# Feed-forward with 512-column moving operands and the down projection one output block at a time

## The reference

```python
def swiglu(x, w_gate, w_up, w_down):
    return (jax.nn.silu(x @ w_gate) * (x @ w_up)) @ w_down

x = x + 0.5 * swiglu(rms_norm(x, ffn1_norm[l]), ffn1_w_gate[l], ffn1_w_up[l], ffn1_w_down[l])
...
x = x + 0.5 * swiglu(rms_norm(x, ffn2_norm[l]), ffn2_w_gate[l], ffn2_w_up[l], ffn2_w_down[l])
```

## Time and profile before

| what | value |
|---|---|
| time, median of 3 runs | 1132.12 us (1131.58 to 1132.88) |
| span of the profiled execution | 1131.7 us, 22927 instructions |
| what lies around that span | the execution's own time is not given apart; the median of the runs is 0.4 us above the span |
| PE busy | 1110.8 us, 98% |
| DVE busy | 756.4 us, 67% |
| ACT busy | 572.3 us, 51% |
| POOL busy | 81.4 us, 7% |
| mean granted TensorE clock | 0.995 of full speed (2.4 GHz) |
| weight stream | 369 blocks of 512 KB, median 3.5 us from issue to landing |

### The profile page before, as it was taken

One profiled execution on the slowest core, in us unless ns is written; L12 is line 12 of the kernel. 1 busy time (PEld: TensorE's weight loads), 2 busy tenths in 40 slices (PEclk: granted clock), 3 DMA queues, 4 the chain that ended last, 5 costly groups with the idle time before them and its releaser, 6 DMA issues.

```text
span 1131.7 us, 22927 instructions
## 1 busy us (share of the span) xinstructions
PE 1110.8 (98%) x8842; PEld 1086.0 (96%) x8842; DVE 756.4 (67%) x1113; ACT 572.3 (51%) x798; POOL 81.4 (7%) x75
## 2 busy tenths in 40 slices
PE   9999999998999999999999999999999999999997
PEld 7999999787999999999999998999999999999997
DVE  6756566887795656677656567677856668565654
ACT  6544444664664444455444445534655555444443
POOL 3200000226010000020000002000200011000000
PEclk9999999999999999999999999999999999999998
DMA  8755555453256555546555554555555546555551
GB/s 281 261 186 169 186 184 185 160 166 103 94 183 190 174 189 182 178 142 214 185 184 170 191 179 158 186 176 176 184 189 178 183 149 205 187 185 186 168 185 38
DMA packets 55570, 200.04 MB, mean 177 GB/s; under 512 B 6304, under 2 KB 6304, under 8 KB 55392
## 3 DMA queue, kind: packets, MB, share of 16 engines
q1 hardware_dynamic: 54576, 196.11, 52.8%
q0 software_dynamic: 512, 2.65, 0.6%
q10 hardware_dynamic: 432, 0.57, 0.2%
HBM read 198.26 MB, written 1.05 MB: 176 GB/s over the span
## 4 chain that ended last, share of the span: by engine, by line
PE 91%; DVE 5%; POOL 1%; ACT 1%; DMA 1%; issue 0%; ACTq 0%; DVEq 0%; POOLq 0%
PE bank L1087 30%; PE bank L1089 29%; PE bank L1088 29%; DVE x_lo L722 2%; DVE w_lo L716 1%; DVE x L733 1%; PE bank L1281 1%; DMA x<-x_in 1%; POOL x_sq L372 1%; POOL x_sq L364 1%; PE bank L1291 0%; PE bank L1347 0%; POOL qk_a L355 0%; PE bank L1302 0%; PE bank L1144 0%
## 5 line engine op out<-in xcount | busy, mean ns | idle before, releaser
L716 DVE TENSOR_TENSOR w_lo<-w_raw,w_hi 128x1024 fp32r<-128x1024 f32 x369 | 466.2, 1272 | 248.7 <-ACT w_hi L415 248.1
L1087 PE MATMUL bank<-x_hi,w_hi 128*128 128x256 f32 x1792 | 509.1, 284 | 4.2 <-DVE x_lo L722 2.3
L1088 PE MATMUL bank<-x_lo,w_hi 128*128 128x256 f32 x1792 | 507.1, 283 | 0.0
L1089 PE MATMUL bank<-x_hi,w_lo 128*128 128x256 f32 x1792 | 507.1, 283 | 0.0
L415 ACT ACTIVATE w_hi<-w_raw 128x1024 fp32r<-128x1024 f32 x369 | 386.1, 1053 | 236.0 <-PE bank L1089 226.1
L1087 PEld LDWEIGHTS bank<-x_hi,w_hi 128*128 128x128 f32 x1792 | 343.9, 192 | 6.5 <-DVE w_lo L716 2.5
L1088 PEld LDWEIGHTS bank<-x_lo,w_hi 128*128 128x128 f32 x1792 | 343.9, 192 | 0.1
L1089 PEld LDWEIGHTS bank<-x_hi,w_lo 128*128 128x128 f32 x1792 | 343.9, 192 | 0.0
L1087 PE MATMUL bank<-hid_hi,w_hi 128*128 128x256 f32 x704 | 199.2, 283 | 0.0
L1088 PE MATMUL bank<-hid_lo,w_hi 128*128 128x256 f32 x704 | 199.2, 283 | 0.0
L1089 PE MATMUL bank<-hid_hi,w_lo 128*128 128x256 f32 x704 | 199.2, 283 | 0.0
(11 more groups left out here) (183 smaller groups left out, 947.5 us busy)
## 6 DMA issues: line engine op xcount, KB each, us to landing
w_raw<-stream SPq DMA_DIRECT2D x369, 512.0 KB, 3.5
const<-const_in POOLq DMA_DIRECT2D x1, 1248.0 KB, 7.8
w_raw<-stream SPq DMA_DIRECT2D x4, 256.0 KB, 5.8
out<-x_sq SPq DMA_DIRECT2D x4, 256.0 KB, 2.7
rows<-rows_in POOLq DMA_DIRECT2D x1, 576.0 KB, 9.8
x<-x_in ACTq DMA_DIRECT2D x2, 256.0 KB, 5.8
x<-x_in SPq DMA_DIRECT2D x2, 256.0 KB, 6.9
sgu_w<-sgu_w_in POOLq DMA_DIRECT2D x1, 512.0 KB, 11.5
```

Of the source, the lines that this page charges most:

```text
L716: nc.vector.tensor_tensor(w_lo[:, slot, :], w_raw[:, slot, :], w_hi[:, slot, :].bitcast(F32), ALU.subtract).then_inc(w_split, 1)
L1087: nc.tensor.matmul(dst, a_hi, b_hi, start=first, stop=False, skip_group_check=True)
L1088: nc.tensor.matmul(dst, a_hi, b_lo, start=False, stop=False, skip_group_check=True)
L1089: return nc.tensor.matmul(dst, a_lo, b_hi, start=False, stop=last, skip_group_check=True)
```

## The change

The sums stay the same, apart from the place where `rstd` and the 0.5 are multiplied in.

- **Moving operand.** High and low part of an activation lie side by side (`x_hl`, `hid_hl`), and `both` takes the place of `three` in the feed-forward: one matmul of the high weight with 512 columns (high and low activation), and one of the low weight with the 256 high columns, added into the left half of the bank. A bank now holds the high sum in its left half and the low sum in its right half; gate and up of one hidden block are a pair of banks.
- **Reading a result.** ScalarE copies the two right halves (`fetch`), VectorE adds them to the left halves and scales the gate part alone (`add`); silu and product follow, then `hid_hi` on ScalarE. `hid_lo` moves from VectorE to GpSimd (`hidden_lo`). The up part is no longer scaled by `rstd`; the output is.
- **Order.** All 44 gate and up blocks come first, then 22 down blocks in a new layout, in which output block m needs 22 tiles: 2.75 blocks. Output block m is finished, read (`output`: reduce over the two halves, scale by 0.5 and `rstd`, add to x), split and squared, while TensorE works on the next ones.
- **Start of the next phase.** After a feed-forward the x_hi, x_lo and squares are made one block at a time. After a mixer they come in pairs as before. Squares and their additions are now 128x256 each (seven additions for three of 512 and one of 256). `split(n + 2)` of a phase stands at the end of the phase before. ScalarE's split of block 7 comes ahead of its root.

```diff
-                for b in range(3, 7):
+                for b in range(3, 8):
                     split(n0 + b)
                 rms_root(p)
+
+                def fetch(f, j, i=0):
+                    act.wait_ge(w_used, n0 + 2 * f + 2 + 8 * i)
+                    nc.scalar.activation(low_s[:], pair[j][:, :, S:2 * S], ACT.Copy).then_inc(low_copied, 1)
...
+                def step(f, i=0):
+
+                    fetch(f - 2, f % 4, i)
+                    split(n0 + 2 * f + 2, i, 8)
+                    split(n0 + 2 * f + 3, i, 8)
+                    gate(4 * i + (f - 2))
+                    hidden(f - 2, i)
...
+                def add(f, j):
+
+                    dve.wait_ge(low_copied, FC * e + 1 + f)
+                    nc.vector.tensor_tensor(sum_s, pair[j][:, :, 0:S], low_s[:], ALU.add).then_inc(parts_added, 1)
+                    dve.wait_ge(parts_added, FC * e + 1 + f)
+                    nc.vector.tensor_tensor(gate_s, gate_s, rstd[:], ALU.mult).then_inc(gate_scaled, 1)
...
+                def step(f, i=0):
+
+                    split(n0 + 2 * f + 2, i, 8)
+                    add(4 * i + (f - 2), f % 4)
+                    split(n0 + 2 * f + 3, i, 8)
+                    product(4 * i + (f - 2), f % 2)
...
+                def output(m):
+
+                    if DOWN_ENDS[m]:
+                        dve.wait_ge(w_used, n0 + UP_B + DOWN_LAST[m] + 1)
+                    else:
+                        dve.wait_ge(down_done, (KC - 2) * e + m + 1 - sum(DOWN_ENDS[:m]))
+                    y_s = y_b[:, m % 2, :]
+                    nc.vector.tensor_reduce(y_s, bank[m % 4].rearrange("p (a s) -> p s a", a=2), AX.X,
+                                            ALU.add).then_inc(down_read, 1)
+                    dve.wait_ge(down_read, KC * e + m + 1)
+                    nc.vector.scalar_tensor_tensor(y_s, y_s, 0.5, rstd[:], ALU.mult, ALU.mult).then_inc(y_scaled, 1)
+                    dve.wait_ge(y_scaled, KC * e + m + 1)
+                    nc.vector.tensor_tensor(x[:, m, :], x[:, m, :], y_s, ALU.add).then_inc(x_new, 1)
...
+            def hidden_lo(e):
+
+                for f in range(FC):
+                    pool.wait_ge(hid_hi_done, FC * e + f + 1)
+                    nc.gpsimd.tensor_tensor(hid_lo[:, f, :], hid_b[:, f % 2, :], hid_hi[:, f, :].bitcast(F32),
+                                            ALU.subtract).then_inc(hid_split, 1)
...
+            def both(dst, a_hi, a_lo, b_hl, first, last):
+
+                nc.tensor.matmul(dst, a_hi, b_hl.rearrange("p a s -> p (a s)"), start=first, stop=False, skip_group_check=True)
+                return nc.tensor.matmul(dst[:, 0:S], a_lo, b_hl[:, 0, :], start=False, stop=last, skip_group_check=True)
...
+                for m in range(KC):
...
+                    for k in range(FC):
+                        tile = FC * m + k
+                        n, w = n0 + UP_B + tile // KC, slice(tile % KC * P, (tile % KC + 1) * P)
+                        if tile % KC == 0:
+                            pe.wait_ge(w_split, n + 1)
+                        if m == 0:
+                            pe.wait_ge(hid_split, FC * e + k + 1)
+                        last = both(bank[m % 4][:, :], w_hi[:, n % RING, w], w_lo[:, n % RING, w], hid_hl[:, k, :, :], k == 0,
+                                    k == FC - 1)
```

More of the change, by code:

```diff
@@ L471, in chunk, with hidden @@
[L471 to L478, removed]
+                def hidden(f, i=0):
+                    act.wait_ge(hid_done, FC * e + 1 + f + 4 * i)
+                    nc.scalar.activation(hid_hi[:, bass.ds(4 * i + f, 1), :], hid_b[:, f % 2, :].unsqueeze(1),
+                                         ACT.Copy).then_inc(hid_hi_done, 1)
@@ new lines, in step @@
+                def step(f, i=0):
[4 more added lines that the diff above has]
+                    hidden(f - 2, i)
+                for f in range(2):
+                    fetch(f, (f + 2) % 4)
+                    split(n0 + 8 + f)
+                    gate(f)
+                    hidden(f)
+                for f in range(4, LEAD):
+                    step(f)
@@ L480, in ffn @@
                 with act.Fori(0, LOOPED // 4) as i:
                     for j in range(4):
[L482 to L485, removed]
-                gate(FC - 1)
-                hidden(FC - 1, (FC - 1) % 4)
-                split(n0 + FFN_B + 1)
+                        step(LEAD + j, i)
+                fetch(FC - 2, FC % 4)
+                split(n0 + UP_B + 2)
+                gate(FC - 2)
@@ L802, in ffn @@
+                def step(f, i=0):
[3 more added lines that the diff above has]
+                    product(4 * i + (f - 2), f % 2)
+                for f in range(2):
+                    add(f, (f + 2) % 4)
+                    split(n0 + 8 + f)
+                    product(f, f, e > 0)
+                for f in range(4, LEAD):
+                    step(f)
                 with dve.Fori(0, LOOPED // 4) as i:
@@ L814, in attention_mixer @@
+                for b in range(1, FC):
+                    split(n0 + UP_B + b + 3)
+                    for m in range(KC - 1):
+                        if DOWN_LAST[m] == b - 1:
+                            output(m)
+                        if DOWN_LAST[m] == b - 2 and p < 5:
+                            input_lo(p + 1, m)
+                output(KC - 1)
+                if p < 5:
+                    input_lo(p + 1, KC - 1)
             def attention_mixer(n0, p):
-                for b in range(2, 6):
+                for b in range(3, 6):
```

325 lines of the change are left out of this document (166 added, 159 removed).

## The result

The changed kernel takes 1142.34 us (median of 4 runs, 1139.71 to 1143.76), the kernel before 1132.50 beside it: ratio 1.0085, interval 1.0071 to 1.0099. Measured once more later it was 1140.86 against 1133.23, 1.0064 (1.0048 to 1.0081). It is slower, by 8 to 10 us; forecast were 2. The profiled execution took 1143.76, with a span of 1141.9.

A forecast was written before the change was run, and what follows sets the result against it. TensorE, 98% busy, was taken to bound the kernel before. Its 1131.7 us span, plus 6.9 in the feed-forwards, less 4.7 from early outputs, gave 1133.9 of span, stated as 1134 us, range 1118 to 1150.

The forecast's parts named there:

- The wider operand: Feed-forward matmuls: a weight tile takes 347 ns in place of 360, 27 us less over four feed-forwards.
- The third rival: Feed-forward tiles stay near 357 ns, so the wide matmul saves less than said: 1140 us, chance 0.06.
- The closed loop: Up phase: ScalarE and VectorE queues need 5.67 to 5.76 us per output, against TensorE's 5.55, so matmuls wait.
- the jump back: Up phase, where the hardware loop jumps back: ScalarE's next instruction starts 0.47 us later, three times.
- 155 tiles that remain are 53.8 us at full rate: Down phase, after the wait for hid_lo at tile 21: the remaining tiles run at full rate, 53.8 us.
- the 8 us of waiting: TensorE waits for GpSimd's hid_lo at the last hidden blocks, about 8 us together with earlier waits.
- Given back: Early output blocks shorten both mixers' starts (-1.8, -1.9 us) and the very end (-1.0): -4.7 us in all.
- Only the last four wait for the last block: Very end: of 32 small matmuls only four wait for the last output block, some 2.7 us: -1.0 us.
- The first (a faster round): Up phase: queues overlap more, a round takes 5.55 us: 1120 us, in the extreme 1099; chance 0.22.
- The second (GpSimd against VectorE): Up phase: hid_lo on GpSimd collides with VectorE's splits, up to 0.7 us a round: 1150 us, chance 0.12.
- The fourth, small things: Extra waits per round, late weight blocks at the first feed-forward, outputs holding back splits: 1143 to 1150 us, chance 0.10.
- the likeliest case: Whole kernel: the forecast itself, 1134 us, spread over 1127 to 1141, with chance 0.50.

The follow-up runs named there:

- with one more copy: Changed kernel plus a second ScalarE copy of each output's low parts out of PSUM, into a buffer not read then: 1184.14 us, ratio 1.0450.
- with the add first: Changed kernel with VectorE's add and gate scaling moved ahead of both weight splits in the up phase: 1105.93 us, ratio 0.9764; again 1105.52.
- The run with filled waits: Changed kernel plus 6 and 12 unused 512-column matmuls on TensorE before its waits for hid_lo of hidden blocks 20 and 21: 1137.69 us, ratio 1.0039.
- add first, copied twice: Changed kernel with add and gate scaling ahead of both up-phase splits, and ScalarE copying each output's low parts twice: 1111.93 us, ratio 0.9821.
- first of the two runs with three matmuls: Changed kernel, its order kept, with each tile again three 256-column matmuls: 1145.92 us, ratio 1.0110; output wrong.

## Why the prediction was nearly right, point by point

- **The wider operand.** 347 ns was right as the lower of two values; the other is 353. The mean over an up phase was 349 to 355 ns (122.68 and 124.80 us for 352 tiles, with the short stalls at its start), so the third feed-forward without the loop was 184.98 us and not 183.3. At 353 the stretch from tile 21 to the end is 54.9 and not 53.8. Three matmuls took 4.5 us more than two in the 352 tiles of an up phase at 347, the 13 ns a tile that I took, and 1.05 us more in the 176 tiles of a down phase at 353, 6 ns a tile, half of it. The third rival had 2.5 ns a tile, from the gap formula of the Trainium skill ("TensorE: Matmul & The Clock Gate", Back-to-back issue gap); both values are above it.
- **The closed loop** was right to 0.01 us, hop by hop, and is now shown and not only argued: 5.77 us, 6.26 with one more copy, 4.73 with the add first. Only the jump back was mis-sized: a round with one took 5.79 to 5.84 us, so 0.02 to 0.07 more and not 0.47, three times. That is why tile 21 came at 137.4 us (third), 138.6 (second and fourth) and 140.3 (first), 1.2, 1.5 and 0.6 sooner than forecast.
- **What failed** is the step "155 tiles that remain are 53.8 us at full rate". It measured 57.5, 55.8, 56.5, 56.4: 11.0 us more over four. About 9 of that is the granted clock at 1.2 GHz behind the wait, and about 2 the spacing of tiles. For behind the slow stretch the first and the fourth feed-forward went on at 353 ns a tile, the second and the third at 347. TensorE, ten tiles each, first and third feed-forward:
```profile
165.28 0.40 PE L1155 MATMUL pair<-wide,w_hi 128*128 128x512 f32 x1
...
168.81 0.40 PE L1155 MATMUL pair<-wide,w_hi 128*128 128x512 f32 x1
```
```profile
665.34 0.39 PE L1155 MATMUL pair<-wide,w_hi 128*128 128x512 f32 x1
...
668.81 0.39 PE L1155 MATMUL pair<-wide,w_hi 128*128 128x512 f32 x1
```
155 tiles are 54.8 us at the one and 53.7 at the other, so the slow clock cost 2.7, 2.1, 2.7 and 1.6 us. The run with filled waits, all at 353, gave 6.7 of these 9 back. I had named the 8 us of waiting and never asked what a wait of that length does to the clock. The first feed-forward was hit most, +5.6 for 2.7: its clock was at half for the whole 6 us, and its tiles came at 353.
- **The errors partly cancelled.** By spans the forecast was 1133.9 and the result 1141.9, 8.0 us more: +11.0 here and +1.9 at the end, less the 4.8 us by which tile 21 came sooner in the four feed-forwards, mostly because I had priced the jump back too high. With that term right the forecast would have been about 1129. So it is in part luck that the total lies this near. (The 0.4 us that I put between span and time is 1.8 to 2.1 in the profiles whose own time is on record.)
- **Given back.** Both mixers as forecast, 1.9 and 1.8. The end was wrong in size, and in this profile in sign. "Only the last four wait for the last block" overlooked TensorE's queue: all 32 stand behind the last product, and 28 of them take about as long as the last block's sum, scaling, add and square (2.3 us). So the sums take the 3.63 us of the earlier trace rows anyway, and 12.1 us pass behind the last product in five of the profiles, 12.5 before: 0.4 us given back. In the two profiles of the changed kernel it was 13.4 and 12.7. The clock falls behind the last product in every profile, the kernel before included, there 4.0 us on; in the first of these two it fell 2.1 us on, while the small matmuls still ran, and the sums took longer:
```profile
1128.46 4.91 PE L1477 MATMUL pair<-ones,x_sq 128*128 128x1 f32 x32
```
- **The rivals.** The first (a faster round) was wrong for this order, but its extreme, 1099, is within 7 us of what the kernel does when one line moves: 1105.9. I had the number and asked only whether the rows might show more overlap, not which order would give it. The second (GpSimd against VectorE) fell: 0.65 us stayed free between them, and the run with hid_lo on VectorE was the same. The Trainium skill's remark on the shared access ("GPSIMD Engine Reference", Specifications) is not contradicted; in the loop the two never worked at once. The fourth, small things, is nearest to what happened in size, though one thing of about 9 us is not small.
- **In sum:** forecast 1134, measured 1142.3 and 1140.9; direction right, in the range of 1118 to 1150, at the edge of the likeliest case (1127 to 1141). The forecast of 2 us more lay itself within the 2.3 that I had called no change; what came is four to five times as much.

## What to carry to other kernels

Engines that are 53% and 67% busy can set the pace: follow one output around all in-order queues, add the start-to-start times, and compare the sum with what the bounding engine needs. If the loop is longer, look for the instruction on it that could stand elsewhere in its queue (here the two splits between a copy and its next use) before counting on anything that speeds up the bounding engine; a saving there was worth 3.6 us with the loop and 21.9 without it. And price a wait of several microseconds in TensorE's stream at its length plus the slower tiles behind it, here some 2 us behind waits of 1.56 and 2.97.

## What the runs showed of the hardware

- After one tile in 5 us the granted clock was at 1.2 GHz for 3 to 6 us behind the wait, in all eight stretches of the changed kernel's two profiles; it cost 1.6 to 2.7 us each time. It fell in all four behind a single wait of about 2.9 us as well (three matmuls a tile), in none behind a single wait of 1.0 to 1.4 us (add first, copied twice), and in none with the waits filled by matmuls.
- A pair of a 512- and a 256-column matmul, at the same granted clock, came either 347 or 353 ns apart from the next. Nearly always one value held from one interruption of the stream to the next, and which one it was differed between executions of one program; three matmuls of 256 columns took 360. Why is open.
- One-column matmuls of 128x128 weights put between the tiles of a wide stream cost 0.106 us each (28 for 3.0 us), nearly as much as at the end by themselves (32 in 3.6).
- Starting accumulation in the second half of a bank while the first half had just begun to accumulate gave a wrong output (first of the two runs with three matmuls); with one start for both halves it was whole. That the second start wiped the first half is the likely reason; the two runs also differ in a stop flag.
